# Cross-attention's values with queries as columns, shares turned apart from the heads, all query passes ahead of the scores, and two low-part splits handed from VectorE to GpSimd

## The reference, cut to what matters

```
q = (rms_norm(x) * g) @ wq          # 256 x 256: four heads of 64
k, v = (rms_norm(mem) * g) @ wkv    # 256 memory rows
s = q @ k.T / 8 ; p = softmax(s)    # per head, 256 x 256
o = p @ v                           # 256 x 64 per head
x = x + rms_norm(o @ wo) * g        # wo: 256 x 1024
x = x + rms_norm(relu(h @ w1)**2 @ w2) * g   # the MLP behind it, 4096 wide
```

## Time and profile before

| what | value |
|---|---|
| median of 3 runs | 1373.96 us (1373.23 to 1374.51) |
| the profiled execution, its own time | 1373.97 us |
| its span | 1372.2 us |
| PE busy | 1360.3 us (99%) |
| PE weight loads busy | 1136.3 us (83%) |
| DVE, ACT, POOL busy | 1011.9, 745.4, 98.0 us |
| granted TensorE clock | 1.00 in every stage shown below |

### The profile page before, as it was taken

One profiled execution on the slowest core, in us unless ns is written; L12 is line 12 of the kernel. 1 busy time (PEld: TensorE's weight loads), 2 busy tenths in 40 slices (PEclk: granted clock), 3 DMA queues, 4 the chain that ended last, 5 costly groups with the idle time before them and its releaser, 6 DMA issues.

```text
span 1372.2 us, 19438 instructions
## 1 busy us (share of the span) xinstructions
PE 1360.3 (99%) x7455; PEld 1136.3 (83%) x7455; DVE 1011.9 (74%) x1518; ACT 745.4 (54%) x1155; POOL 98.0 (7%) x104
## 2 busy tenths in 40 slices
PE   9999999999999999999999999999999999999998
PEld 6887888888888878888888778888888868888886
DVE  5666878777764777977787777886677876886665
ACT  4564555555445655555455666654445675654443
POOL 0000011000000000211111001020000001200000
PEclk9999999999999999999999999999999999999999
DMA  9844455555565335666655424368866533366552
GB/s 305 247 149 153 157 174 191 184 187 192 174 214 184 125 121 166 226 206 205 205 194 157 160 93 138 124 207 235 211 192 211 161 105 124 123 198 196 190 189 88
DMA packets 146578, 242.26 MB, mean 177 GB/s; under 512 B 4603, under 2 KB 91403, under 8 KB 146222
## 3 DMA queue, kind: packets, MB, share of 16 engines
q1 hardware_dynamic: 142498, 226.97, 51.1%
q0 software_dynamic: 3712, 13.77, 3.7%
q10 hardware_dynamic: 276, 0.27, 0.1%
HBM read 239.03 MB, written 1.97 MB: 176 GB/s over the span
## 4 chain that ended last, share of the span: by engine, by line
PE 93%; DVE 4%; ACT 1%; issue 1%; DMA 0%; POOL 0%; ACTq 0%; DVEq 0%
PE ps L1105 19%; PE ps L1069 16%; PE ps L1078 15%; PE ps L1075 15%; PE ps L1110 10%; PE ps L1213 3%; PE ps L1276 2%; PE ps L1291 2%; PE ps L1322 1%; PE ps L1887 1%; DVE wlo L2526 1%; PE ps L1310 1%; PE ps L1149 1%; PE ps L1153 1%; PE ps L1152 1%
## 5 line engine op out<-in xcount | busy, mean ns | idle before, releaser
L2526 DVE TENSOR_TENSOR wlo<-raw,whi 128x1024 fp32r<-128x1024 f32 (+2 forms) x427 | 532.8, 1259 | 190.1 <-ACT whi L2009 188.8
L2009 ACT CAST whi<-raw 128x1024 fp32r<-128x1024 f32 (+1 forms) x431 | 445.5, 1043 | 260.8 <-PE ps L1078 158.0
L1105 PE MATMUL ps<-act,whi 128*128 128x512 f32 x1152 | 315.5, 394 | 0.0
L1069 PE MATMUL ps<-whi,mhi 128*128 128x512 f32 (+2 forms) x688 | 236.6, 393 | 0.7 <-DVE mlo L2553 0.7
L1078 PE MATMUL ps<-whi,mlo 128*128 128x512 f32 (+2 forms) x688 | 231.4, 385 | 0.0
L1075 PE MATMUL ps<-wlo,mhi 128*128 128x512 f32 (+2 forms) x688 | 231.2, 385 | 0.0
L1105 PEld LDWEIGHTS ps<-act,whi 128*128 128x128 f32 x1152 | 199.4, 189 | 28.9 <-DVE act L2556 0.4
L1110 PEld LDWEIGHTS ps<-act,wlo 128*128 128x128 f32 x1152 | 177.6, 189 | 25.0
L1110 PE MATMUL ps<-act,wlo 128*128 128x256 f32 x1152 | 184.2, 281 | 0.0
L1078 PEld LDWEIGHTS ps<-whi,mlo 128*128 128x128 f32 x688 | 129.2, 188 | 26.6
L1075 PEld LDWEIGHTS ps<-wlo,mhi 128*128 128x128 f32 x688 | 129.3, 188 | 26.5 <-DVE wlo L2526 0.5
(11 more groups left out here) (322 smaller groups left out, 1549.8 us busy)
## 6 DMA issues: line engine op xcount, KB each, us to landing
raw<-in_mlp_w SPq DMA_DIRECT2D x64, 1024.0 KB, 5.3
raw<-in_w_up SPq DMA_DIRECT2D x44, 1024.0 KB, 5.2
raw<-in_w_in SPq DMA_DIRECT2D x38, 1024.0 KB, 5.1
raw<-in_w_down SPq DMA_DIRECT2D x22, 1024.0 KB, 5.1
raw<-in_ev_w_in SPq DMA_DIRECT2D x10, 1024.0 KB, 5.1
raw<-in_w_out SPq DMA_DIRECT2D x8, 1024.0 KB, 5.0
raw<-in_xa_wkv SPq DMA_DIRECT2D x4, 1024.0 KB, 5.2
raw<-in_ev_w_out SPq DMA_DIRECT2D x4, 1024.0 KB, 5.4
```

The source lines that it names most:

```text
L1069: nc.tensor.matmul(o, hi[:, kx, rows_], wh[:, k, c0:c0 + w], start=first and h == 0 and k == 0 and (tt == 0 or at[1] == 0), stop=False)
L1105: nc.tensor.matmul(both, wh[:, k, w], act2[:, kx].rearrange("p i n -> p (i n)"), start=kx == 0, stop=False)
L2009: nc.scalar.copy(whi[:, m % HL, 0:w], raw[:, n % RAW, h * w:h * w + w]).then_inc(hi_done, 1)
L2526: nc.vector.tensor_tensor(wlo[:, m % HL, 0:w], raw[:, n % RAW, h * w:h * w + w], whi[:, m % HL, 0:w].bitcast(F32), ALU.subtract).then_inc( ...
```

## The change

The values are now computed with the queries as columns: v (64 columns) is stationary, the turned exponents are 128 moving columns, and the two heads of a pair go to PSUM rows 0 to 63 and 64 to 127 (`column_values`, line 1313, which the odd layer's own attention uses already). So the heads come out already transposed, and they are not turned again. What is turned instead are the shares (the reciprocals of the exponents' sums): VectorE takes them (`weights_out`), GpSimd spreads each over 64 columns, `turn_shares` transposes them on TensorE, VectorE copies them out (`shares_out`) and multiplies (`scale_heads`). The high and low parts are then taken from SBUF. `query(1, (3,))` stands ahead of the first scores; `turn(0)` stands behind the last ones. The low parts of halves n0+13 and n0+14 are GpSimd's, and its first waits until VectorE has done n0+12. Copies of pair 2 and pair 3 change engines.

```diff
-            plan.group(("ox", l, tt), "split")
+            plan.group(("ox", l, tt), "dve")
...
-                           lambda s, i=i: kvn[:, s, 256 + HD * i:256 + HD * i + HD], i, lambda qt, i=i: (6 + qt, HD * i), False))
+                           lambda s, i=i: kvn[:, s, 256 + HD * i:256 + HD * i + HD], i, lambda qt, i=i: (6 + qt, P * (i // 2)), False))
...
-                d["columns"] = k[0] == "odd"
+                d["columns"] = k[0] in ("odd", "cross")
...
-                    eng = (("dve", "dve", "dve", "act") if d["deep"] else ("act", "dve", "dve", "dve"))[i // 2 % 4]
+                    eng = (("dve", "dve", "act", "dve") if d["deep"] else ("act", "dve", "dve", "dve"))[i // 2 % 4]
...
-        low_by_pool = sorted([2 * plan.jobs["w1", l, 1][0] + h for l in range(DEPTH) for h in range(2)])
+        low_by_pool = sorted([2 * plan.jobs["w1", l, 1][0] + h for l in range(DEPTH) for h in range(2)] +
+                             [2 * plan.jobs["wo", l][0] + 1 for l in range(DEPTH)] + [2 * plan.jobs["w1", l, 0][0] for l in range(DEPTH)])
...
                     sp.wait_ge(hi_done, 2 * (n - RAW + 1))
                     wait_lo(sp, 2 * (n - RAW) + 1)
+                    if (2 * (n - RAW) in low_by_pool) != (2 * (n - RAW) + 1 in low_by_pool):
+                        wait_lo(sp, 2 * (n - RAW))
...
                     if key == "yx":
+                        wait_lo(pool, 2 * plan.jobs["wo", l][0])
+                        split_low(2 * plan.jobs["wo", l][0] + 1)
+                        split_low(2 * plan.jobs["w1", l, 0][0])
+                        for tt in range(TT):
+
+                            pool.wait_ge(cross_weights, TT * l + tt + 1)
+                            nc.gpsimd.tensor_copy(cross_spread_at(tt).rearrange("p (h d) -> p h d", h=HX),
+                                                  rden[:, tt, 0:HX].unsqueeze(2).to_broadcast([P, HX, HD])).then_inc(cross_spread, 1)
...
-                def turn_cross(tt):
-
-                    pe.wait_ge(o_ready, o_counts["cross", l] - 1 + tt)
-                    turn_blocks(("ox", l, tt), [o_nat[:, tt, b * P:(b + 1) * P] for b in range(2)])
+                def turn_shares(tt):
+
+                    pe.wait_ge(cross_spread, TT * l + tt + 1)
+                    turn_blocks(("ox", l, tt), [cross_spread_at(tt)[:, b * P:(b + 1) * P] for b in range(2)])
...
-                query(1, (2,))
+                query(1, (2, 3))
...
                 scores(0)
                 scores(2)
-                query(1, (3,))
                 turn_query(1)
-                both_of(turn, 0)
                 pe.wait_ge(grp_dve, plan.by_number[plan.groups["qkx", l, 2]][2])
                 scores(4)
                 scores(6)
+                both_of(turn, 0)
                 both_of(turn, 1)
                 both_of(values, 0)
                 both_of(turn, 2)
+                turn_shares(0)
                 both_of(values, 1)
                 both_of(turn, 3)
                 both_of(values, 2)
-                turn_cross(0)
+                turn_shares(1)
                 both_of(values, 3)
-                pe.wait_ge(grp_dve, plan.by_number[plan.groups["ox", l, 0]][2])
+                pe.wait_ge(cross_low, TT * l + 1)
                 cross_out(0, 0)
-                turn_cross(1)
                 cross_out(0, 1)
-                pe.wait_ge(grp_dve, plan.by_number[plan.groups["ox", l, 1]][2])
+                pe.wait_ge(cross_low, TT * l + 2)
...
-                split_half(n0 + 12)
+                split_half(n0 + 13)
 
                 act.wait_ge(rstd_ready, rs_count["xx", l])
...
-                split_half(n0 + 13)
                 key = ("qkx", l, 1)
                 group_ready(act, key)
...
+                split_half(n0 + 14)
                 us, u0 = units_of["cross", l], first_unit["cross", l]
...
                 def cross_hi(tt):
 
-                    key = ("ox", l, tt)
-                    group_ready(act, key)
-                    nc.scalar.copy(mhi[:, 0:2, tt * P:tt * P + P], ps[:, bank_of(key), 0:SEQ].rearrange("p (b n) -> p b n", b=2)).then_inc(grp_act, 1)
+                    act.wait_ge(cross_scaled, TT * l + tt + 1)
+                    nc.scalar.copy(cross_block(mhi, tt), by_block(cross_heads_at(tt))).then_inc(cross_high, 1)
...
+                copied(2)
                 cross_hi(0)
...
-                split_half(n0 + 13)
+                split_half(n0 + 12)
                 us, u0 = units_of["cross", l], first_unit["cross", l]
...
+                def weights_out(tt):
+
+                    dve.wait_ge(at_e, u0 + HX * (tt + 1))
+                    nc.vector.reciprocal(rden[:, tt, 0:HX], den[:, tt, 0:HX]).then_inc(cross_weights, 1)
+
+                def shares_out(tt):
+
+                    key = ("ox", l, tt)
+                    group_ready(dve, key)
+                    nc.vector.tensor_copy(cross_shares_at(tt), group_bank(key)[:, 0:SEQ]).then_inc(grp_dve, 1)
+
+                def scale_heads(tt):
+
+                    dve.wait_ge(grp_dve, plan.by_number[plan.groups["ox", l, tt]][2])
+                    dve.wait_ge(at_o, u0 + HX * (tt + 1))
+                    nc.vector.tensor_tensor(cross_heads_at(tt), ps[:, 6 + tt, 0:SEQ], cross_shares_at(tt), ALU.mult).then_inc(cross_scaled, 1)
...
+                query_out()
                 lows(0)
+                query_turned()
                 lows(1)
-                query_out()
-                copied(0)
                 lows(2)
                 lows(3)
+                weights_out(0)
+                copied(0)
                 copied(1)
-                copied(2)
-                norm_out(("cross", l), 0, HX, heads_of(o_nat, 0, 0, HX), HX)
-                split_half(n0 + 14)
+                shares_out(0)
+                scale_heads(0)
+                weights_out(1)
+                copied(3)
                 cross_lo(0)
-                norm_out(("cross", l), HX, HX, heads_of(o_nat, 1, 0, HX), TT * HX)
+                shares_out(1)
+                scale_heads(1)
+                cross_lo(1)
                 split_half(n0 + 15)
-                cross_lo(1)
```

More of the change, by code:

```diff
@@ L418, in build_network @@
         o_ready = sem("o_ready")
+        cross_weights = sem("cross_weights")
+        cross_spread = sem("cross_spread")
+        cross_scaled = sem("cross_scaled")
+        cross_high = sem("cross_high")
+        cross_low = sem("cross_low")
         heads_out = sem("heads_out")
@@ L694, in build_network @@
             order += [("dsa", l)] if l % 2 == 0 else []
-            order.append(("cross", l))
         o_counts = {k: 2 * (i + 1) for i, k in enumerate(order)}
@@ L802, in index_banks, with cross_heads_at, cross_spread_at, cross_shares_at @@
             return bank_of(key), (6, 7, 6, 7, 6, 7, 7, 7)[t]
+        def cross_heads_at(tt):
+            return o_nat[:, tt, 0:256]
+        def cross_spread_at(tt):
+            return o_nat[:, tt, 256:512]
+        def cross_shares_at(tt):
+            return o_nat[:, tt, 512:768]
+        def cross_block(t, tt):
+            return t[:, 0:2, tt * P:tt * P + P]
+        def by_block(t):
+            return t.rearrange("p (b n) -> p b n", b=2)
         def group_ready(eng, key):
@@ L2419, in _, with copied @@
                                          bias=low[:, d["qt"], s:s + 1], accum_out=den[:, d["qt"], s:s + 1]).then_inc(at_e, 1)
-                split_half(n0 + 14)
-                act.wait_ge(at_x, u0 + 8)
-                act.wait_ge(at_o, u0 + 2)
-                nc.scalar.copy(values_of(u0 + 6, us[6], True), turned_pair(u0 + 6, us[6])).then_inc(at_ya, 1)
+                def copied(p):
+                    u, d = u0 + 2 * p, us[2 * p]
+                    act.wait_ge(at_x, u + 2)
+                    act.wait_ge(at_o, u - 4)
+                    nc.scalar.copy(values_of(u, d, True), turned_pair(u, d)).then_inc(at_ya, 1)
                 def cross_hi(tt):
-                    key = ("ox", l, tt)
-                    group_ready(act, key)
-                    nc.scalar.copy(mhi[:, 0:2, tt * P:tt * P + P], ps[:, bank_of(key), 0:SEQ].rearrange("p (b n) -> p b n", b=2)).then_inc(grp_act, 1)
+                    act.wait_ge(cross_scaled, TT * l + tt + 1)
+                    nc.scalar.copy(cross_block(mhi, tt), by_block(cross_heads_at(tt))).then_inc(cross_high, 1)
                 def cross_square(tt, c):
@@ L3339, in query_out, with query_turned @@
                     nc.vector.tensor_scalar(proj[:, 1, 0:256], ps[:, 7, 0:256], rstd[:, NORM["xx", l], 1:2], None, ALU.mult).then_inc(q1_ready, 1)
+                def query_turned():
                     key = ("qkx", l, 2)
@@ L3343, in query_out @@
                                             ALU.mult).then_inc(grp_dve, 1)
-                def cross_lo(tt):
[L3347 to L3351, removed]
+                def weights_out(tt):
[9 more added lines that the diff above has]
```

(5 more changed lines are left out.)

## The result

The changed kernel takes 1376.27 us (median of 13 runs, 1374.75 to 1377.74); the kernel before, in the same rounds, 1373.89 (1373.23 to 1375.16). The ratio is 1.0016, its interval 1.0009 to 1.0023: slower by about 2.4 us, within the 0.2% that the prediction called no change, and 0.9 us above the forecast of 1375.4. The profiled execution took 1376.96 us with a span of 1375.2 us, 3.0 us more than the span before.

What follows compares the result with a forecast made beforehand. TensorE, 99% busy, was taken to bound the kernel. Per layer, +0.92 us before the output products less 0.19 gave +0.73; twice is +1.46, rounded to +1.4, so 1375.4 us. Own range 1374.4 to 1377.0; with rivals 1372.4 to 1377.6.

Steps and rivals of the forecast that it cites:

- Queries moved forward: Query step 3 ahead of the first scores on TensorE: six products delay `scores(0)` by 0.72 us.
- Copy of pair 0 behind the late minima: On VectorE, `copied(0)` queues behind minima that wait for two exponents, so `values(0)` starts 1.64 us late.
- Column form: TensorE's values step per pair takes 0.59 us instead of 0.84; 0.26 saved, less about 0.07 per tile-shape change.
- Shares: Turned reciprocals before `cross_out`: GpSimd's spread takes 0.39 us, hidden for tile 0, +0.04 us for tile 1.
- No turn between the output products: On TensorE, `cross_out(0, 1)` follows `cross_out(0, 0)` by 1.46 us instead of 1.65: 0.19 gained.
- Splits, and GpSimd beside VectorE: GpSimd's two 2.41 us low-part splits are hidden and don't slow VectorE: charged nothing, bound above 0.5 us per layer.
- Rival 2: GpSimd's long splits hold VectorE's minima in the cross-attention stage: +4.4 us, 1378.4 us; chance 0.11.
- Rival 1: No exponent or minimum holds TensorE, first `cross_out` 1.73 us early: -3.8 us over two layers, 1370.1 us; chance 0.07.
- +0.73 a stage: Forecast net delay at the end of `cross_out` per layer: +0.92 us less 0.19.

Runs made afterwards that it cites:

- the repetition: The changed kernel with nothing altered, timed once more beside the kernel before: 1375.62 us (11 runs), ratio 1.0015.
- the kernel that undoes it: The changed kernel with turn 0 back ahead of scores 4 and copy 0 ahead of the third minimum, queries left ahead: 1373.11 us, ratio 0.9993.
- the kernel with the columns alone: The changed kernel with only column values and turned shares kept; order and splits as in the kernel before: 1372.78 us, ratio 0.9988.
- the splits alone: The kernel before, with the low parts of n0+13 and n0+14 given to GpSimd and ScalarE's splits placed as changed: 1373.95 us, ratio 0.9997.
- fillers: Five products nobody reads, behind the second queries' turn: 1375.30 us (1.0006) in the changed kernel, 1376.94 us (1.0019) in the kernel before with only the order changed.
- the order alone: The kernel before with all query passes ahead of the scores and turn 0 behind scores 6, values in the old form: 1377.04 us, ratio 1.003.

## Why the prediction was right, point by point

Its mechanism held, and one term was missing. Set from the first scores on, in us: forecast, the profile with the clock kept (the repetition), the profile with the clock lost.

| step | forecast | clock kept | clock lost |
|---|---|---|---|
| scores 4 | 2.64 | 2.74 | 2.73 |
| scores 6 | 3.78 | 3.67 | 3.67 |
| values 0 | 6.12 | 6.02 | 6.01 |
| first output product | 10.19 | 10.17 | 11.08 |
| end of the output products | 15.83 | 15.75 | 16.66 |

- *Queries moved forward*: +0.72 forecast for `scores(0)`; from the first product of query step 2 it is 1.61 us (869.71 to 871.32) against 0.90 before (869.81 to 870.71), so +0.71.
- *Copy of pair 0 behind the late minima*: the step on which the forecast turned. Right by size (values 0 at 6.01 for 6.12), and shown as the cause by the kernel that undoes it (values 0 at 4.89), but together with the turn's place: the prediction laid it to the minima alone, and by the estimate above they hold the copy for some 0.3 us and the turn behind scores 6 for 0.8.
- *Column form*: 0.59 a pair as forecast. From values 0 to the first output product it is 4.15 us with the clock kept, where the forecast had 4.07 with the shares' waits, and 4.79 before. In the kernel with the columns alone it is 4.33, and the turn of x began there 0.48 us behind the start of the last output product instead of 0.23, with VectorE's two splits still between the output tiles: 0.34 us a stage are left of the 0.95 of the terms (0.76 + 0.19), so the 1.5 us by which that kernel is faster aren't accounted for by them.
- *Shares*: GpSimd's spread took 0.40 us (0.39 taken). TensorE turned the second shares at 881.45, 0.04 us behind the place where it would have (880.82 + 0.59).
- *No turn between the output products*: 5.58 us for the block (882.40 to 887.98) against 5.83, so 0.25 instead of 0.19.
- *Splits, and GpSimd beside VectorE*: nothing, as charged. Rival 2 is refuted by the minima's 0.68 to 0.69 us and by the splits alone. The Trainium skill, SBUF — State Buffer, Who interferes with whom, has a reduction never contend with GpSimd on this chip; the trace agrees, with these numbers.
- *Rival 1 (TensorE's own pace)*: not so; two waits of 1.23 or 1.24 and 0.23 us stand in every profile of this order without fillers. The second was forecast at 0.6, so scores 6 came 0.1 us early.
- *The missing term*: the sum took the granted clock to be 1.00 throughout, as it was before. In the profiled execution the low level cost 11.08 - 10.17 = 0.91 us a stage, 1.8 us in all; the medians of the two series are 1376.27 and 1375.62. The runs with a mean clock of 0.999 lie at the forecast (1374.75 to 1375.66 in the first series, 1375.07 to 1375.62 in the second); one run of the first with 1.000 doesn't (1376.54). With the forecast's +0.73 a stage against (15.75 + 0.71) - 15.82 = +0.64 measured, the rest of the sum is within 0.2 us for both stages.

So the forecast of a small loss was right for its own reason, and most of the 0.9 us between it and the first median is the share of executions that lose the clock: the five of these thirteen runs at 0.999 or more have a median of 1375.55, the eight others one of 1376.42. That the median stayed inside the range although this term was missing is owed to the width of the range. That the fall follows the 1.24 us of idle, and that filling them keeps the clock, rests on the two pairs of this order with and without fillers (in all, 16 runs of 31 without them at 0.998 or lower, none of 22 with them). Without this order a mean clock of 0.998 or lower is rare: 2 of the 84 runs of the kernel before that stand beside the experiments, and 1 of the 66 runs of the other variants, where the low level lay at the kernel's start. Why the same idle leads to it in some executions, in one stage and not the other, and why it lasts 3.4 us in one kernel and at least 13.5 in another, stays open: no run changed what TensorE does behind the idle time alone.

## What to carry to other kernels

Where engines work through steps in a written order, look at what each step stands behind: a turn and its copy, whose exponents were ready early, were queued behind scores and minima that waited for another engine's exponents, and that cost more than the cheaper products brought. Moving work ahead of a wait takes away what filled it; ask what fills it now, and price the idle time with the array's clock as well as with its length. When a median moves by more than the sum, sort the runs by their mean clock before looking for another wait, and look in a trace for the place where the clock was low.

## What was not expected of the hardware

- An idle time of 1.24 us on TensorE, with short operations around it (busy 1.52 of 2.75 us), was followed by the clock's lower level for about 3.4 us, though the engine was then busy without a gap; before, an idle of 0.65 us in the same place was not, in its profile. The low level can pass unseen where it is hidden: the eight transposes took 1.69 us instead of 1.10, and nothing came later for it, since VectorE's copy was the later of the two.
- In another kernel (the order alone) the low level lasted at least 13.5 us with TensorE busy in all of them, in one of two like stages, and cost 5 us.
- Whether it happens differs between executions of one program, so its cost shows as a spread: in the order alone 1376.54 to 1382.15 without fillers (7 runs), 1375.88 to 1378.11 with them (11 runs).
- VectorE's reductions from PSUM took 0.69 us beside GpSimd's splits, and 1.29 for two as in the kernel before, where none ran beside them, while its squares from SBUF took 1.7 us when they met a split, against a median of 1.22.
